# Feed-forward products of tile pairs by seven half-size products instead of eight

## The reference, cut to what matters

```
h = rms_norm(x, norm_ffn_pre_g)                       # first block, stage 1
f = (silu(h @ w_gate) * (h @ w_up)) @ w_down          # D_FF = 2816
x = x + rms_norm(f, norm_ffn_post_g)

def swiglu(h, w_gu, w_down):                          # second block, stages 2 and 5
    gate, up = jnp.split(h @ w_gu, 2, axis=-1)        # D_FF_2 = 2816
    return (jax.nn.silu(gate) * up) @ w_down
x = x + 0.5 * swiglu(rmsnorm(x, ffn1_norm), ffn1_w_gu, ffn1_w_down)
...
x = x + 0.5 * swiglu(rmsnorm(x, ffn2_norm), ffn2_w_gu, ffn2_w_down)
```

## Time and profile before

| | us |
|---|---|
| median of 3 runs | 1945.75 (1945.31 to 1946.38) |
| the profiled execution's own time | 1944.65 |
| its span, first to last instruction | 1942.9 |
| PE busy in it | 1922.1 |
| DVE, ACT, POOL busy | 1003.3, 757.4, 241.0 |
| granted PE clock, mean of full speed | 0.998 |

### The profile page before, as it was taken

How to read it: one execution, slowest core, us unless ns; L and a number is a source line. 1 busy time by engine, 2 the same in 40 slices (tenths; PEclk the granted TensorE clock), 3 DMA queues, 4 the chain that set the end, 5 groups by cost and what they waited for, 6 DMA issues and landing times.

```text
span 1942.9 us, 23941 instructions
## 1 busy us (share of the span) xinstructions
PE 1922.1 (99%) x9634; PEld 1564.8 (81%) x9634; DVE 1003.3 (52%) x1503; ACT 757.4 (39%) x1171; POOL 241.0 (12%) x242
## 2 busy tenths in 40 slices
PE   9999999999999999999999999999999999999998
PEld 7777788878888888788888888777787788888887
DVE  6677535373334345733333366887754454334335
ACT  6344533453223233432322356665543343233224
POOL 6210001201011011010110112222010011011010
PEclk9999999999999999999999999999999999999999
DMA  6122233433333323333333232222232233333323
GB/s 175 57 66 66 62 96 103 119 98 98 98 97 98 98 85 111 92 96 96 97 98 98 81 110 70 66 66 66 87 98 64 77 96 95 96 95 96 97 60 104
DMA packets 340767, 176.32 MB, mean 91 GB/s; under 512 B 6481, under 2 KB 339378, under 8 KB 340658
## 3 DMA queue, kind: packets, MB, share of 16 engines
q1 hardware_dynamic: 340658, 174.79, 30.8%
HBM read 172.67 MB, written 2.10 MB: 90 GB/s over the span
## 4 chain that ended last, share of the span: by engine, by line
PE 92%; DVE 4%; ACT 2%; issue 1%; DMA 1%; POOL 0%; SPq 0%; ACTq 0%; DVEq 0%
PE ps L1122 28%; PE ps L1126 28%; PE ps L1124 28%; PE ps L1189 1%; PE ps L1169 1%; PE ps L1178 1%; PE ps L1274 1%; PE ps L1135 1%; PE ps L1292 1%; DVE WL L1589 1%; PE ps L1203 1%; PE ps L1159 0%; DVE TS L1640 0%; PE ps L1152 0%; DVE L L1690 0%
## 5 line engine op out<-in xcount | busy, mean ns | idle before, releaser
L1122 PE MATMUL ps<-HH,WH 128*128 128x512 f32 x1728 | 686.2, 397 | 0.5 <-ACT HH L1345 0.4
L1126 PE MATMUL ps<-HL,WH 128*128 128x512 f32 x1728 | 674.7, 390 | 0.9 <-DVE HL L1610 0.8
L1124 PE MATMUL ps<-HH,WL 128*128 128x512 f32 x1728 | 674.1, 390 | 0.7 <-DVE WL L1589 0.7
L1589 DVE TENSOR_TENSOR WL<-RAW,WH 128x1024 fp32r<-128x1024 f32 (+3 forms) x335 | 400.3, 1197 | 530.1 <-ACT WH L1335 529.7
L1335 ACT ACTIVATE WH<-RAW 128x1024 fp32r<-128x1024 f32 (+3 forms) x335 | 337.6, 1010 | 518.4 <-PE ps L1126 514.5
L1122 PEld LDWEIGHTS ps<-HH,WH 128*128 128x128 f32 x1728 | 324.6, 188 | 75.8 <-issue 8.7
L1126 PEld LDWEIGHTS ps<-HL,WH 128*128 128x128 f32 x1728 | 324.5, 188 | 71.5 <-DVE HL L1610 2.1
L1124 PEld LDWEIGHTS ps<-HH,WL 128*128 128x128 f32 x1728 | 324.7, 188 | 70.5 <-issue 4.1
L1122 PE MATMUL ps<-GH,WH 128*128 128x512 f32 x688 | 269.6, 392 | 0.0
L1126 PE MATMUL ps<-GL,WH 128*128 128x512 f32 x688 | 268.4, 390 | 0.0
L1124 PE MATMUL ps<-GH,WL 128*128 128x512 f32 x688 | 268.2, 390 | 0.0
(11 more groups left out here) (214 smaller groups left out, 1535.4 us busy)
## 6 DMA issues: line engine op xcount, KB each, us to landing
RAW<-in_ffn_w_gu SPq DMA_DIRECT2D x88, 512.0 KB, 3.8
RAW<-in_w_in SPq DMA_DIRECT2D x67, 512.0 KB, 3.7
RAW<-in_ffn_w_down SPq DMA_DIRECT2D x32, 512.0 KB, 3.9
RAW<-in_w_gate SPq DMA_DIRECT2D x22, 512.0 KB, 3.8
RAW<-in_w_up SPq DMA_DIRECT2D x22, 512.0 KB, 3.8
RAW<-in_w_out SPq DMA_DIRECT2D x16, 512.0 KB, 4.2
RAW<-in_mem_w_kv SPq DMA_DIRECT2D x16, 512.0 KB, 3.9
RAW<-in_w_down SPq DMA_DIRECT2D x16, 512.0 KB, 4.1
```

The costliest lines, as they stand in the source:

```text
L1122: e.matmul(bk, wh, xh, start=k == 0, stop=False)
L1124: e.matmul(bk, wl, xh, start=False, stop=False)
L1126: last = e.matmul(bk, wh, xl, start=False, stop=k == kt - 1)
L1589: e.tensor_tensor(at.weight(n, "L"), m["RAW"][:, n % NRAW, 0:kt, :], at.weight(n, "H").bitcast(F32), ALU.subtract).then_inc(*sg.inc("lo", n))
```

## The change

Two neighbouring tiles f, f+1 of gate (or of up) are a pair, and the pair's product is taken as a 2 by 2 block product: the depth of 1024 in two halves (chunks 0 to 3 and 4 to 7), the 256 output columns in two tiles, and the 512 positions in two halves. Instead of eight half-size block products seven are made (Winograd's form of Strassen's scheme), over sums of the blocks. A product has 4 chunks and 256 positions: 12 matmuls.

- Pairs are `PAIRS = ((4, 6), (0, 2, 5), (0, 2, 4))` of the three thirds: 8 pairs, each with a gate and an up slot, 16 slots in each of the three stages. Tiles 0 to 3 of the first third (`PLAIN`) and tiles 4 and 7 of the second are done as before, tile by tile.
- **Weights**: of the 7 weight operands 4 are sums or differences of half tiles (POOL, `combine_weights`, four 128x512 operations per slot, into `TS` tiles) and 3 are half tiles as loaded. Each is split by ACT and DVE as before, in halves of 128x512: 7 per slot where there were two of 128x1024. The rings `WH` and `WL` are counted in 6 halves. Combinations are planned up to 8 weight items ahead (`LOOK`), over at most one whole tile.
- **Activations**: seven operands too. DVE makes the finished h (with R, `normal`), POOL makes four mixed blocks of each chunk pair (`mix`, four 128x256 operations for each of 4 chunks), ACT and DVE split them into `NH` and `NL` (`mix_split`), in three groups during tiles 0 to 2 (`MIX_AT`). After the last plain tile `HH` and `HL` are overwritten by the finished h (`place`), chunk by chunk.
- From then on R is already in h: plain tiles lose `normed` and `gate_r` (`gate_plain`: Silu straight from PSUM).
- **Results**: five banks per slot. DVE adds banks and partial sums in 128x256 operations (`sum_one` to `sum_four`, `corner`), ACT copies one bank and takes Silu, POOL multiplies gate and up (`gate_mixed`). Product 5 adds onto the bank of product 2, after ACT copied it; product 6 onto the bank of product 1, after DVE's second sum of it. The pair's G chunks are split after the first two products of the next slot.
- `NH` and `NL` lie where scores, masks and other constants lie, so masks and fills for the second block are made later, in stage 2's last down products (`LATE`), and only a few at the start.

```diff
+MIX_AT = ((0,), (1, 2), (3,), ())
+PLAIN = len(MIX_AT)
+PAIRS = ((4, 6), (0, 2, 5), (0, 2, 4))
+LOOK = 8
+MIXED = (("b", 2), ("c", 0), ("a", "11"), ("e", 1), ("d", 3), ("a", "21"), ("c", "22"))
...
+    def weigh_pair(self, key, name, c0):
+        n, r = len(self.weights), len(self.raws)
+        self.raws += [(name, 0, KD, c0 + P), (name, 0, KD, c0)]
+        self.weights += [("sum", key, 2), ("sum", key, 1), ("half", r + 1, 0), ("sum", key, 3), ("half", r, 1), ("half", r + 1, 1),
+                         ("sum", key, 4)]
...
+        self.needs += [r + 1] * 7
+        self.spent += [r] * 4 + [r + 1] * 2 + [r + 2]
+        self.raw_done[r] = (("lo", n + 4), ("comb", (key, 3)))
+        self.raw_done[r + 1] = (("lo", n + 2), ("lo", n + 5), ("comb", (key, 4)))
...
+    def pair(self, gen, G, f, up, name, c0, pending):
+        key = (G, f, up)
+        n = self.weigh_pair(key, name, c0)
+        ta, tb = ("gt", (G, f)), ("gt", (G, f + 1))
+        self.ahead(n)
+        for i, (b, op) in enumerate(MIXED):
+            if i < 5:
+                self.bank(("pr", key, b))
+            self.step("product", gen, key, i, n + i)
+            if i < 2 and pending:
+                self.split_tile(*pending.pop(0))
+            elif i == 2:
+                self.tiles.take(("u", key))
+                self.step("sum_one", key, n)
+                self.banks.give(("pr", key, "b"), ("part_sum", ("u2", key)))
+            elif i == 3:
+                self.tiles.take(("w", key) if up else tb)
+                self.step("sum_two", key, n)
...
+            elif i == 6:
+                self.step("sum_four", key, n)
...
+            self.ahead(n + i + 1)
...
+    def product(gen, key, i, n):
+        b, op = MIXED[i]
+        bk = at.bank(("pr", key, b))[:, 0:256]
...
+        if i < 5:
+            wait_all(at.bank_free(("pr", key, b)))
+        elif i == 5:
+            g.wait_ge(*sg.at("gate_act", ("s1", key)))
+        else:
+            g.wait_ge(*sg.at("part_sum", ("c22", key)))
+        for c in range(4):
...
+            g.wait_ge(*sg.at("hi", n))
+            g.wait_ge(*sg.at(hi, ready))
+            e.matmul(bk, wh[:, c, :], xh, start=i < 5 and c == 0, stop=False, skip_group_check=i >= 5)
+            g.wait_ge(*sg.at("lo", n))
+            e.matmul(bk, wl[:, c, :], xh, start=False, stop=False, skip_group_check=i >= 5)
+            g.wait_ge(*sg.at(lo, ready))
+            o = e.matmul(bk, wh[:, c, :], xl, start=False, stop=c == 3, skip_group_check=i >= 5)
+        o.then_inc(*sg.inc("mm", n))
...
+    def sum_two(key, n):
+        u, home = at.tile(("u", key)), mixed_b(key)
+        g.wait_ge(*sg.at("part_sum", ("u2", key)))
+        g.wait_ge(*sg.at("mm", n + 3))
+        e.tensor_tensor(u[:, 0:256], at.bank(("pr", key, "e"))[:, 0:256], u[:, 256:512], ALU.add).then_inc(*sg.inc("part_sum", ("u3", key)))
+        g.wait_ge(*sg.at("part_sum", ("u3", key)))
+        wait_all(at.tile_free(home))
+        e.tensor_tensor(at.tile(home)[:, 256:512], at.bank(("pr", key, "c"))[:, 0:256], u[:, 0:256], ALU.add).then_inc(
+            *sg.inc("part_sum", ("c22", key)))
...
+    def combine_weights(key, j):
+        ra, rb = plan.pair_raws[key]
+        a, b = m["RAW"][:, ra % NRAW, :, :], m["RAW"][:, rb % NRAW, :, :]
+        out = at.raw_sum(key, j)
+        x, y, op = {1: (b[:, 0:4, :], b[:, 4:8, :], ALU.add), 2: (at.raw_sum(key, 1), a[:, 0:4, :], ALU.subtract),
+                    3: (a[:, 0:4, :], b[:, 0:4, :], ALU.subtract), 4: (a[:, 4:8, :], at.raw_sum(key, 2), ALU.subtract)}[j]
...
+    def gate_mixed(key, a):
+        G_, f, _ = key
+        t, w = (at.tile(("gt", (G_, f + 1))), at.tile(("w", key))) if a else (at.tile(("gt", (G_, f)))[:, 256:512],
+                                                                              at.tile(("u", key))[:, 256:512])
+        g.wait_ge(*sg.at("part_sum", ("c21" if a else "c12", key)))
+        g.wait_ge(*sg.at("gate_act", ("silu", (G_, f, 0), a)))
+        e.tensor_tensor(t, t, w, ALU.mult).then_inc(*sg.inc("gm", (key, a)))
```

More of the change, by code:

```diff
@@ L381, in pipeline, with normal, mix @@
             step()
-    def ffn(self, gen, gate, g0, up, u0, down, evac, third0):
-        R = None
+    def normal(self, gen, c, gcol):
+        self.tiles.take(("N", gen, c))
+        self.step("normal", gen, c, gcol + c, self.norm(gen))
+    def mix(self, gen, f, gcol):
+        for c in MIX_AT[f]:
+            self.normal(gen, c, gcol)
+            self.normal(gen, c + 4, gcol)
+            for a in range(2):
+                self.tiles.take(("mix", gen, c, a))
+            self.step("mix", gen, c)
@@ new lines, in mix_split, with place @@
+    def mix_split(self, gen, f):
+        for c in MIX_AT[f]:
+            for a in range(2):
+                self.step("mix_split", gen, c, a, self.mixed_free)
+                self.tiles.give(("mix", gen, c, a), ("op_lo", (gen, c, a)))
+    def place(self, gen):
+        n = len(self.weights) - 1
+        self.by_chunk.add(n)
+        for c in range(KD):
+            self.step("place", gen, c, ("mm", ("k", n, c) if c < KD - 1 else n))
+            self.tiles.give(("N", gen, c), ("xl", ("H", ("n", gen), c)), ("mixed", (gen, c % 4, 3)))
@@ L416, in ffn @@
                 self.tiles.give(("gt", key), ("xl", ("G", G, f)))
+                if f < PLAIN - 1:
+                    self.mix(gen, f, gcol)
+            while pending:
+                self.split_tile(*pending.pop(0))
             if n == 2:
-                self.end_norm(gen, ("pj", ("gt", (G, nf - 1))), ("gr", (G, nf - 1)))
+                self.hfree = self.mixed_free = (done,)
+                for half in range(2):
+                    self.held["L", half] = self.held["PT", half] = (done,)
             if n == 2 and gen == 5:
@@ L425, in ffn @@
                 evac(n, mt, b, mm)
-                self.split_to(len(self.weights) + NSPL)
+                if n == 2 and gen == 2:
+                    for i in LATE[mt]:
+                        self.step("consts", i, done)
+                self.ahead(len(self.weights))
             self.gfree = (mm,)
@@ L602, in gate @@
             return gates[br, mt]
-        consts = iter(range(9))
+        consts = iter(range(2))
         def more_consts():
@@ L898, in second_block @@
         self.out_proj(5, "mem_w_o_2", 8, COL["ffn2_norm_2"], [step, None, lambda: turned(3), None, step])
+        self.mixed_free = sum((self.held[b, half] for b in ("L", "PT") for half in range(2)), ())
+        self.mixed_free += (("go", 3), ("go", 2), ("at", (3, 7)), ("dB", 3))
         self.half_ffn(5, "ffn2_w_gu_2", "ffn2_w_down_2", None, 9)
@@ L1328, in split @@
     def split(n, free):
-        kt = plan.weights[n][2]
-        g.wait_ge(*sg.at(f"d_raw{n % NRAW}", n))
+        kind, a, b, *_ = plan.weights[n]
+        if kind == "sum":
+            g.wait_ge(*sg.at("comb", (a, b)))
+        else:
+            r = a if kind == "half" else plan.raw_index[n]
+            g.wait_ge(*sg.at(f"d_raw{r % NRAW}", r))
         if len(plan.weights[n]) > 4:
             wait_all(free)
-        elif n >= NSPL:
-            g.wait_ge(*sg.at("mm", n - NSPL))
-        e.activation(at.weight(n, "H"), m["RAW"][:, n % NRAW, 0:kt, :], ACT.Copy).then_inc(*sg.inc("hi", n))
+        else:
+            for i in plan.owners[n]:
+                g.wait_ge(*sg.at("mm", i))
@@ new lines, in split, with mix_split, place @@
+        e.activation(at.weight(n, "H"), at.raw(n), ACT.Copy).then_inc(*sg.inc("hi", n))
+    def mix_split(gen, c, a, free):
+        g.wait_ge(*sg.at("mixed", (gen, c, 2 + a)))
+        wait_all(free)
+        e.activation(m["NH"][:, 2 * a:2 * a + 2, c, :], blocks(at.tile(("mix", gen, c, a)), 256), ACT.Copy).then_inc(*sg.inc("op_hi", (gen, c, a)))
+    def place(gen, c, free):
+        g.wait_ge(*sg.at("N", (gen, c)))
+        g.wait_ge(*sg.at(*free))
+        e.activation(m["HH"][:, c, :], at.tile(("N", gen, c)), ACT.Copy).then_inc(*sg.inc("xh", ("H", ("n", gen), c)))
```

352 lines of the change are left out of this document (288 added, 64 removed).

## The result

The changed kernel takes 2015.62 us (median of 4 runs, 2014.00 to 2017.26) against 1946.07 for the kernel before on the same chip (4 runs, 1945.31 to 1947.69): a ratio of 1.0356, 95% interval 1.0338 to 1.0374. The prediction was 1916.6 us (range 1906 to 1935). It was wrong in sign and size.

A forecast was written before the change was run, and what follows sets the result against it. TensorE was taken as the bound, by number of matmuls times pitch. The terms -38.4 + 6 + 2.0 + 1.2 = -29.2 us, from the median 1945.75, gave 1916.6 us, with 1906 to 1935 for 8 in 10.

The forecast's parts named there:

- TensorE's part: Pair slots: 84 matmuls at 0.120 take 10.08 us instead of 10.88, over 48 slots 38.4 us less.
- (b): First four tiles of each stage: normal, mix and place work mostly covered, 0.4 us each, 1.2 in all.
- The term for product 6: Product 6 waits for VectorE's sum in slots following an up slot: 0.5 us at 12 places, 6 us.
- The estimate of 89%: VectorE and GpSimd together, holding each other, need 18.0 of 20.16 us per two slots, so it fits.
- Engines: Whole-kernel busy times: GpSimd 241 + about 250 us, VectorE near 1003 + 160.
- (f): TensorE's clock: waits of half a microsecond at a time should not lower it; no cost.
- (a): After the last up slot of a six-tile third, down products wait for G chunk 4: 1.0 us twice, 2.0.
- (c): Masks and reset moved from the start to the second stage's down products: between 0 and -1.8 us, taken as 0.
- (e): SP's DMAs: the same bytes, two DMAs per 10.08 instead of 10.88 us; off the path.
- The rival "slower": Every GpSimd operation holds VectorE, slots of 12.35 us, 2016; by the skill's rule 11.6, 1980. Chance 0.09 in all.
- "right": Signs: slots 10.1 us, TensorE waiting only in products or first G chunks, some 10 us; split subtractions 0.69 to 1.8.
- "wrong": Signs: WH or WL waits in most slots, pitch over 0.122, or product 0 waiting for combinations or DMA.

The follow-up runs named there:

- e2: Changed kernel with six plain tiles instead of four at the head of each stage and the first pair at tile 6: 1986.57 us.
- e10: Changed kernel with the first third of each stage in eight plain tiles and no pair, later thirds keeping their pairs: 1966.75 us.
- e8: Changed kernel with gate_r on VectorE instead of GpSimd, nothing else: 2011.95 us.
- e13: Changed kernel with mixes cut to 16 of 256 columns, their splits reading the finished h (mixed operands left out): 1999.51 us.
- e5: Changed kernel with weight combinations cut to 8 of each 128 columns, splits of the summed weights reading a fixed tile: 1946.71 us.
- e9: Changed kernel with six plain tiles at each stage's head, look-ahead 2, and combinations and gate_r on VectorE: 1969.69 us.
- e6: Changed kernel with each weight combination replaced by GpSimd fills that read nothing from SBUF, weight sums left out: 1960.78 us.

## Why the prediction was wrong, point by point

- **TensorE's part, -38.4: right.** A slot is 84 x 0.120: 10.07 to 10.08 us wherever nothing holds it, a product 1.44.
- **The step that failed most is (b), the start of a stage.** Put at 0.4 us per stage, it was 17.8 for the slot and 1.25 before it, 57 us in the three stages where the sum has 1.2. The 43.5 us of cover counted time before R; 29 us were left, the loads in it were taken at lengths without the port (0.60 for what took 0.93 to 1.04 on average), and the chain through ScalarE, GpSimd and VectorE was costed as a sum of busy times, with no order. "Place follows the last plain tile chunk by chunk" was the part that plain tiles can't mend: e2 has 21.8 us more cover and `place` is still 4.7 us late, behind `gate_r` and `gate_up`. e10, with the down products in between, shows the term at zero; e8, e13 and e5 show that no one part of it would have been enough to drop.
- **The term for product 6, 12 x 0.5 = 6 us, named the right wait and mis-sized it.** Fifteen gate slots were late, not 12 (slot 8, behind a plain tile, as well), and they lost 1.1 to 6.9 us each, 48.2 with the up slots behind them. Product 5's wait for ScalarE's copy (L1599, 14.2 us in 13 times), which the change had beside it, was nowhere in the sum; in the later slots, which hold 9.5 of it, it comes from the same late gate products, because ScalarE's G split, which waits for them (4.45 us in slot 12), stands in front of the copy. GpSimd ended the gate products 5.2 us into slot 12, not 2.5: the combinations in front of them began 8.5 us into slot 11 (705.40), not at 6, and were stretched (1.44 to 1.74 for 1.29); VectorE then had its splits at up to 1.77. The estimate of 89% for both engines together spoke of averages and missed this. Around slot 12, by window (length, PE, PEld, VectorE, ACT, GpSimd; clock; DMA), VectorE is busy for only 17.96 of 24 us and GpSimd for 14.94:

```profile
700.00:724.00 24.00, 19.50 (x149) 19.09 (x148) 17.96 (x26) 10.26 (x20) 14.94 (x11) 0.93 0.31 88
```

  But the demand comes in one bunch after the landing, and in that bunch there is no slack.
- **Engines.** VectorE 1301.1 for the forecast 1163, GpSimd 572.2 for 491. Of VectorE's 138 us over, 67 are the half splits: 192 at 0.872 and 160 at 0.893 for 0.692. GpSimd's 192 combinations at 1.55 on average for 1.29 are 50 of its 81. Both far from full, as forecast, and both late.
- **(f), the clock, put at nothing: wrong.** The waits reached 7.4 us and did not stop at half a microsecond, and the lower clock cost some 18 us; the edges of the waits, not thought of, some 11. As an average over this kernel a wait cost 1.4 times its idle time (78.2 idle, 29.6 more).
- **(a), 2.0: was 0;** no wait at G chunks of the last third shows. **(c) and (e): as forecast,** no wait of TensorE for the masks; and SP's longer waits, for GpSimd's combinations before a weight tile may be overwritten (17.1 us in 12 times), did not come out as a wait for DMA in TensorE.
- **The rival "slower" gave 2016 and the kernel took 2015.6, but by another way.** It had every slot over, at 12.35 us, in a steady state; in fact 24 of the 48 slots are unstalled, and the sum is made in three first slots, fifteen gate slots and what clock and edges add in them. The near agreement is chance; the mechanism (split subtractions behind combinations) was the right one for the later slots.
- **Its signs.** Pitch, lengths of the split subtractions and the place of the waits (products, for VectorE) came out as for "right", only not "some 10 us in all". Of the signs for "wrong" none showed as named: waits for `WL` were 7.1 us in 6 times, not in most slots. The signs had no line for a wait of the first slot for its activations.
- **The Trainium skill's rule** (SBUF — State Buffer, "SBUF: two separate sides") says that a VectorE operation with two SBUF inputs and a GpSimd one that reads SBUF exclude each other, and that one which only writes does not. The first half was in the prediction, and softened there; e6 agrees with the second half: 153 splits beside fills took 689 ns. For the first half, a split beside GpSimd took 1286 ns on average and one alone 686; the most was 1.83 us.

Left open: how the first slot's 17.8 us divide. Its parts overlap (e5 4.4, e13 3.4, e8 1.7, e2 6.0 each by itself, e9 9.7 for three of them), and were not all taken out together; nor was `gate_up` moved in front of `place` in a kernel whose first pair follows the plain tiles at once. And no run tried back-to-back pairs with a larger ring for VectorE to work ahead in.

## What to carry to other kernels

When work is moved beside a saturated engine, do not add up busy times against the whole stretch: ask from which moment the inputs exist (here R), and walk the queue order through the worst place, with contended lengths. Before adding cover, see whether the late step moves along with it, as `place` did. Spread the new work out: pairs with one plain tile between them lost 4 to 5 us in their later slots, back to back 39. And price a wait of TensorE above its own length, because the clock can go down with it and its edges cost as well.

## What was not expected of the hardware

- GpSimd fills do not hold VectorE (689 ns for a split of 512 columns beside one, 1286 beside operations that read SBUF), so GpSimd's busy time alone says nothing of contention.
- That the hold works in both directions was in the prediction; how much it is over a whole kernel was not. GpSimd's combination went from 1.29 to between 1.51 and 1.64 on average, VectorE's split of 512 columns from 0.69 to as much as 1.83.
- A wait of 4.07 us in a stretch at full clock was followed by matmuls 0.21 apart instead of 0.12 for about 3 us; the waits at the starts of the three stages stand in 13.7 to 17.1 us of low clock each.
- Around each wait busy time is lost besides the idle time, even at full clock: some 11 us over about 50 more waits, 0.2 us each.
